# Distances between steps counted by the pieces' time, the first MLP's chain in three parts, and six seven-product groups more in the second MLP's down-projection

## The reference, cut to what matters

```python
def sq_relu_mlp(h, w1, w2):
    return jnp.square(jax.nn.relu(h @ w1)) @ w2                 # w1: 2048 x 8192
...
up = causal_dwconv(h @ w_up[l], conv_w[l], conv_b[l])           # w_up: 2048 x 11264, 3 taps
y = (jax.nn.gelu(up[..., :D_FF_2], approximate=True) * up[..., D_FF_2:]) @ w_down[l]   # w_down: 5632 x 2048
x = x + rms_norm_2(y, post_ffn_g[l])
```

## Time and profile before

| | us |
|---|---|
| median of 3 runs | 2083.37 (2083.08 to 2083.95) |
| the profiled execution, its own time | 2086.94 |
| its span, first to last instruction | 2085.2 |
| matmul engine busy | 2072.3 (99%), 9250 matmuls |
| VectorE busy | 1350.7 (65%) |
| ScalarE busy | 1117.5 (54%) |
| GpSimd busy | 118.6 (6%) |

### The profile page before, as it was taken

How to read it: one execution, slowest core, us unless ns; L and a number is a source line. 1 busy time by engine, 2 the same in 40 slices (tenths; PEclk the granted TensorE clock), 3 DMA queues, 4 the chain that set the end, 5 groups by cost and what they waited for, 6 DMA issues and landing times.

```text
span 2085.2 us, 23969 instructions
## 1 busy us (share of the span) xinstructions
PE 2072.3 (99%) x9250; PEld 1717.7 (82%) x9250; DVE 1350.7 (65%) x1504; ACT 1117.5 (54%) x1353; POOL 118.6 (6%) x66
## 2 busy tenths in 40 slices
PE   9999999999999999999999999999999999999998
PEld 7888888888888888888888888888888888888887
DVE  6546555666884579666876755566676765576665
ACT  7555654555554455455655554455555544555553
POOL 3000000000000000000002000000111100021110
PEclk9999999999999999999999999999999999999999
DMA  8687666788757776778677777667787756778763
GB/s 298 197 253 233 193 183 221 245 227 262 221 189 222 222 245 208 226 220 229 224 260 234 228 245 231 195 209 221 233 252 253 229 185 211 234 235 257 244 213 120
DMA packets 291906, 469.49 MB, mean 225 GB/s; under 512 B 18512, under 2 KB 82128, under 8 KB 291280
## 3 DMA queue, kind: packets, MB, share of 16 engines
q1 hardware_dynamic: 290928, 463.46, 72.2%
q10 hardware_dynamic: 864, 4.49, 0.6%
HBM read 432.75 MB, written 35.13 MB: 224 GB/s over the span
## 4 chain that ended last, share of the span: by engine, by line
PE 88%; DMA 5%; DVE 3%; ACT 2%; SPq 1%; issue 1%; ACTq 0%; DVEq 0%
PE ps L1734 88%; DMA T<-passed_strip 3%; DVE Wl L1340 1%; DMA passed_strip<-T 1%; DMA passed_rows<-xN 1%; SPq L1041 1%; ACT Wh L1116 1%; DVE T L1443 0%; DMA E<-passed_rows 0%; ACT hid L1219 0%; DVE xN L1469 0%; DVE T L1479 0%; PE ps L1737 0%; SPq L1030 0%; ACT T L1176 0%
## 5 line engine op out<-in xcount | busy, mean ns | idle before, releaser
L1340 DVE TENSOR_TENSOR Wl<-raw,Wh 128x1024 fp32r<-128x1024 f32 x743 | 919.7, 1258 | 565.1 <-ACT Wh L1116 559.7
L1734 PE MATMUL ps<-Wh,aHL 128*128 128x512 f32 x3712 | 1148.5, 390 | 2.1 <-DVE Wl L1335 0.9
L1116 ACT ACTIVATE Wh<-raw 128x1024 fp32r<-128x1024 f32 x743 | 771.5, 1057 | 551.8 <-PE ps L1734 527.8
L1734 PEld LDWEIGHTS ps<-Wh,aHL 128*128 128x128 f32 x3712 | 696.8, 188 | 147.5 <-DVE aHL L1483 1.2
L1734 PE MATMUL ps<-Wl,aHL 128*128 128x512 f32 x1856 | 722.1, 389 | 0.0
L1734 PE MATMUL ps<-Wh,hid 128*128 128x512 f32 x1548 | 480.7, 389 | 3.7 <-DVE Wl L1340 3.7
L1734 PEld LDWEIGHTS ps<-Wl,aHL 128*128 128x128 f32 x1856 | 348.5, 188 | 71.7
L1734 PEld LDWEIGHTS ps<-Wh,hid 128*128 128x128 f32 x1548 | 290.6, 188 | 64.8 <-issue 4.5
L1734 PE MATMUL ps<-Wl,hid 128*128 128x512 f32 x774 | 301.1, 389 | 0.0
L1734 PEld LDWEIGHTS ps<-Wl,hid 128*128 128x128 f32 x774 | 145.3, 188 | 30.1
L1734 PE MATMUL ps<-Wh,oHL 128*128 128x512 f32 x512 | 159.0, 390 | 0.0
(11 more groups left out here) (199 smaller groups left out, 923.0 us busy)
## 6 DMA issues: line engine op xcount, KB each, us to landing
raw<-in_mlp_w_dram SPq DMA_DIRECT2D x256, 512.0 KB, 5.5
raw<-in_w_up_dram SPq DMA_DIRECT2D x176, 512.0 KB, 4.5
raw<-in_sb_w_qkv_dram SPq DMA_DIRECT2D x93, 512.0 KB, 5.1
raw<-in_w_down_dram SPq DMA_DIRECT2D x88, 512.0 KB, 4.6
raw<-in_w_in_dram SPq DMA_DIRECT2D x64, 512.0 KB, 5.2
passed_strip<-T SPq DMA_DIRECT2D x104, 256.0 KB, 4.5
T<-passed_strip SPq DMA_DIRECT2D x208, 128.0 KB, 4.8
raw<-in_sb_w_o_dram SPq DMA_DIRECT2D x32, 512.0 KB, 5.6
```

The source lines that it names most:

```text
L1116: e.activation(Wh[:, i % NW, c], src, ACT.Copy).then_inc(st["hi"][0], 1)
L1340: e.tensor_tensor(Wl[:, i % NW, c], src, Wh[:, i % NW, c].bitcast(F32), ALU.subtract).then_inc(st["lo"][0], 1)
L1734: return e.matmul(o, l, r, start=start, stop=stop, skip_group_check=True)
```

## The change

Three edits. First, `later` counts time instead of pieces: an ordinary piece is four quarters, s0 to s2 are two each and s3 is one (`QUARTERS`), so that inside groups a distance of n spans more pieces. Second, the first MLP's chain: the turn comes one piece later (`behind` 5), and ScalarE's high half and VectorE's low half are steps of their own, each one piece further on. Third, in the second MLP three groups each in the first strip pair of both chunks: `sevens` is also set for s4 = 0, the token sums are also made in the second chunk, the number of ordinary pieces ahead of the first group is 2n - 5 (7 and 5) there and 4 in the second pair of the first chunk (before, 2), the first chunk's fold writes its results, the second's adds to them, and the last sums wait for the fold.

```diff
@@ -21,6 +21,7 @@
 BLOCKS = ((0, 0), (0, 1), (1, 1))
 SPANS = ((slice(0, 128), 0), (slice(128, 384), 4))
 ALL8 = tuple(range(8))
+QUARTERS = {"s0": 2, "s1": 2, "s2": 2, "s3": 1}
 
 
 class Plan:
@@ -47,7 +48,12 @@
         jobs.insert(0 if ahead else len(jobs), job)
 
     def later(self, n, job):
-        self.after(self.at + n, job)
+
+        i, left = self.at, 4 * n
+        while left > 0:
+            i += 1
+            left -= QUARTERS.get(self.pieces[i]["kind"], 4) if i < len(self.pieces) else 4
+        self.after(i, job)
 
 
 def plan_program(sem):
@@ -94,7 +100,7 @@
                                  start=(n == 0, n == 0), last=n == len(ks) - 1, evac=evac, early=None, strip=strips[0]))
         return first
 
-    def strip_pair(w, s4, ks, tail, mov, tiles, evacs, koff=0, sevens=(), fold=None):
+    def strip_pair(w, s4, ks, tail, mov, tiles, evacs, koff=0, sevens=(), fold=None, lead=None):
 
         plain = [kp for kp in ks if kp not in sevens]
         first, n = len(p.pieces), len(plain) - tail
@@ -105,8 +111,8 @@
             p.pieces[first:] = a[:n] + b[:n] + a[n:] + b[n:]
             return first
         b[0]["first"], b[0]["start"] = False, (False, True)
-        lead, gap = (4, 3) if tail else (2, 3 if len(plain) > 7 else 2)
-        rest = a[lead:n] + b[:n] if tail else a[lead:n - 1] + b[:2] + a[n - 1:] + b[2:]
+        lead, gap = (lead or 4, 3 if lead is None or len(plain) > 7 else 2) if tail else (lead or 2, 3 if len(plain) > 7 else 2)
+        rest = a[lead:n] + b[:n] if tail else a[lead:n - 1] + b[:lead] + a[n - 1:] + b[lead:]
         p.pieces[first:] = a[:lead]
         for m, kp in enumerate(sevens):
             seven(w, s4, kp, mov, tiles, (a[0]["strip"], b[0]["strip"]), koff, m, m == 0, fold if m == len(sevens) - 1 else None)
@@ -407,14 +413,23 @@
 
         def f(s, k):
             def landed(moved):
-                turned, hi, lo = done("hid_turned"), done("hid_hi"), done("hid_lo")
+                turned = done("hid_turned")
                 step("turn_strip", to="T1", need=[moved, *free["T1"]], done=turned)
-                step("hid_halves", t0=t0, need=turned, hi=hi, lo=lo)
-                free["T0"], free["T1"] = [turned], [lo]
+                free["T0"], free["T1"] = [turned], [turned]
+                later(1, lambda: high(turned))
+
+            def high(turned):
+                hi, lo = done("hid_hi"), done("hid_lo")
+                step("hid_high", t0=t0, need=turned, hi=hi)
+                free["T1"] = [lo]
+                later(1, lambda: low(turned, hi, lo))
+
+            def low(turned, hi, lo):
+                step("hid_low", t0=t0, hi=hi, lo=lo)
                 if mixed and t0 < 8:
                     free["T1"] = [lo, mix_tokens("hid1", "T1", t0 // 2, 2 if t0 == 0 else 1, [turned])]
                 hid_tiles[t0:t0 + 4] = [lo] * 4
-            trip(s, k, n, "relu", "b", [st["r2"]], landed)
+            trip(s, k, n, "relu", "b", [st["r2"]], landed, 5)
         return f
 
     def load_bias(s, k):
@@ -625,7 +640,7 @@
     MIXED_STRIPS = {0: (0, 2), 8: (2, 1)}
     conv_in = done("conv", 16)
 
-    def evac_conv(j, which, t0, last, at_first):
+    def evac_conv(j, which, t0, last):
         n = next_trip()
 
         def f(s, k):
@@ -666,7 +681,7 @@
                     hi, lo = done("hid_hi"), done("hid_lo")
                     step("gate_high", t0=t0, need=[g, *k], hi=hi)
                     free["E"] = [lo]
-                    if at_first and t0 in MIXED_STRIPS:
+                    if t0 in MIXED_STRIPS:
                         free["E"] = [lo, mix_tokens("hid2", "E", *MIXED_STRIPS[t0], [g])]
                     hid_tiles[t0:t0 + 4] = [lo] * 4
                     if last:
@@ -695,7 +710,8 @@
             for t in range(2):
                 y, q = done("y_summed"), done("y_squared")
                 g = done("y_gained") if s4 < 3 else done("y_gained_last")
-                kw = dict(t=t, s4=s4, set=s, mm=k[t], t0_free=list(free["T0"]), y=y, q=q, g=g, g_row=st["g_row"])
+                kw = dict(t=t, s4=s4, set=s, mm=k[t], t0_free=list(free["T0"]), y=y, q=q, g=g, g_row=st["g_row"],
+                          folded=st.get(("fold", s4)))
                 free["T0"] = [q]
                 st["yg", t, s4] = g
                 if s4 == 2:
@@ -725,14 +741,14 @@
     for c, n in enumerate((6, 5)):
         for j in range(n):
             for which in range(2):
-                i = strip("w_up_2", which * 5632 + (at + j) * STRIP, ALL8, "aHL", tile_hl, evac_conv(at + j, which, 4 * j, j == n - 1, c == 0))
+                i = strip("w_up_2", which * 5632 + (at + j) * STRIP, ALL8, "aHL", tile_hl, evac_conv(at + j, which, 4 * j, j == n - 1))
                 if at + j + which == 0:
                     after(i + 8, lambda: row_norm(into="r6"))
         for s4 in (0, 2):
             i = strip_pair("w_down_2", s4, tuple(range(2 * at, 2 * (at + n))), 0 if s4 else 2, "hid2", hid_tiles,
                            [evac_y(c, s4), evac_y(c, s4 + 1)], koff=2 * at,
-                           sevens=(2 * at, 2 * at + 1, 2 * at + 4) if c == 0 and s4 else (),
-                           fold=fold_into("xn", s4, fresh=True))
+                           sevens=(2 * at, 2 * at + 1, 2 * at + 4) if c == 0 or s4 == 0 else (),
+                           fold=fold_into("xn", s4, fresh=c == 0), lead=4 if s4 else 2 * n - 5)
             if c == 1 and s4 == 0:
                 after(i + 1, gain_rows)
                 after(i + 12, lambda: step("ready_sqrt", need=None))
@@ -1214,7 +1230,7 @@
                     g, oHL = st["g"], oHLs[st["blk"]]
                     e.wait_ge(*st["mm"])
                     e.activation(oHL[:, 4 * g:4 * g + 4, 0:TOK], ps[st["set"]][:, :, 0:TOK], ACT.Copy).then_inc(st["hi"][0], 1)
-                elif k == "hid_halves":
+                elif k == "hid_high":
                     e.wait_ge(*st["need"])
                     e.activation(hid1[:, st["t0"]:st["t0"] + 4, 0:TOK], T1[:, :, :], ACT.Copy).then_inc(st["hi"][0], 1)
                 elif k == "load_bias":
@@ -1502,7 +1518,7 @@
                 elif k == "keep_last":
                     cs = slice(3 * STRIP, 4 * STRIP)
                     e.tensor_tensor(xn[:, 1, cs], ps[st["set"]][:, 1, :], mixed_row[:, cs], ALU.mult).then_inc(st["kept"][0], 1)
-                elif k == "hid_halves":
+                elif k == "hid_low":
                     t0 = st["t0"]
                     e.wait_ge(*st["hi"])
                     e.tensor_tensor(hid1[:, t0:t0 + 4, TOK:2 * TOK], T1[:, :, :], hid1[:, t0:t0 + 4, 0:TOK].bitcast(F32),
@@ -1625,6 +1641,8 @@
                         e.wait_ge(*st["total"])
                         e.tensor_scalar(total, total, 1.0 / 2048, EPS, ALU.mult, ALU.add).then_inc(st["part"][0], 1)
                     e.wait_ge(*st["mm"])
+                    if st["folded"]:
+                        e.wait_ge(*st["folded"])
                     e.tensor_tensor(xn[:, t, cs], xn[:, t, cs], ps[st["set"]][:, t, :], ALU.add).then_inc(st["y"][0], 1)
                     if k == "y_last":
                         mean, r, y, h = moments(half)
```

## The result

The changed kernel takes 2090.39 us (median of 6 executions, 2089.42 to 2091.62), the kernel before 2083.21 beside it (6 executions, 2081.95 to 2083.95): 1.0036 of the time before, 95% interval 1.0025 to 1.0046. It is 7.2 us slower, where +3.3 was forecast with "within 0.2%" as the likeliest case. The profiled execution took 2089.46 us. For a profiled execution, from whose time before all 3.7 us of waits go, the forecast was 2088.4.

What follows compares the result with a forecast made beforehand. The matmul engine, busy 2072.3 of 2085.2 us, was taken as the bound. Terms: -4.1 matmuls, -1.9 first MLP, +5.8 second chunk, +2.5 first chunk, +1.0 clock = +3.3, so 2086.7 us; range 2080.0 to 2090.5.

Steps and rivals of the forecast that it cites:

- within 0.2%: Whole kernel: the forecast and what lies around it, within 4.2 us of before; chance 0.47.
- The matmuls: Second MLP, six more groups: 18 matmuls go at 0.227 us each, 4.1 us saved.
- The first MLP's waits on the median: First MLP: the new order removes waits for VectorE's Wl, 3.7 us in the profile; 1.9 gain taken on the median.
- The second chunk's wait: Second chunk's first pair: low half of hid2 comes late, matmuls wait 5.8 us; bounds 4.3 and 9.1.
- rival 1: Slower: second chunk's GpSimd gate kept out until VectorE stops at the low half, 3.3 us more, 2090.0; chance 0.40.
- The first chunk's wait: First chunk, around the third group: VectorE 0.4 us late plus 2.1 for GpSimd's gate, 2.5; bounds 0.4 and 3.8.
- The clock: Behind the second chunk's 5.4 us wait: half clock may cost 1.0 us; bounds 0 and 2.0.
- The rival "faster": VectorE keeps up, so only the savings stay: 2075.6 to 2079.3 us; needs the 4.3 lower bound wrong; chance 0.13.

Runs made afterwards that it cites:

- before_again: The kernel before, unchanged, measured once more: 2082.95 us; its profiled execution took 2082.79 us.
- low_together: first_mlp_only with the low half of hid1 again right behind its high half, one piece earlier: 2081.89 us, ratio 0.9994.
- first_mlp_only: The kernel before with the new distances and the first MLP's new chain, none of the six added groups: 2083.39 us, ratio 1.0001.
- chunk2_only: The changed kernel without the new groups of the first chunk's first pair, keeping the last chunk's: 2089.76 us, ratio 1.0032.
- lead_one: Changed kernel, last chunk's three groups in its second pair, behind one ordinary piece; two groups in the first chunk's first pair: 2080.76 us, ratio 0.9988.
- after_again: The changed kernel, unchanged, measured once more: 2091.27 us.
- chunk1_only: The changed kernel without the new groups of the second chunk, keeping those of the first chunk's first pair: 2084.11 us, ratio 1.0005.
- fold_behind: The changed kernel with the fold of the last chunk's first pair one piece later, behind the low half of hid2: 2091.80 us, ratio 1.0040.
- chunk2_two: The changed kernel with two groups instead of three in the last chunk's first pair: 2090.80 us, ratio 1.0034.
- table_late: chunk2_two with ScalarE's load of the sqrt table eight pieces later: 2089.37 us, ratio 1.0030.

## Why the prediction was wrong

Set beside before_again's execution, which has no waits for Wl or hid1 in the first MLP, after's span is 6.3 us longer (2087.3 against 2081.0): the matmul engine is busy 2.4 less (2069.9 against 2072.3) and idle 8.7 more. New waits are 8.0 of it: 5.05 for hid2, 2.26 for Wl, 0.7 for hid1. Another 0.6 stands at Wl L1351 in the first 7 us, but the small matmuls of the start are busy 0.6 less there (4.02 us against 4.63), so that it costs nothing. 18 matmuls less give -4.1, the half pace +1.5. That makes 5.4; five stops, each some 0.2 to 0.3 dearer than its row (an estimate from the rows under low_together), make 6.4 to 6.9, against the 6.3 measured. Outside the span after has 0.4 more. With the second dip of 1.7 in half of after's executions the difference is 6.7 to 8.4, and 7.2 is what was measured.

- **The matmuls**, -4.1: right.
- **The first MLP's waits on the median**, "I take the middle, 1.9": this step failed. The prediction saw itself that the profiled execution stood above the median by as much as these waits, and took half of them all the same. An execution near the median had none of them (before_again), and the new chain added two waits for hid1, 0.7 us by their rows and 1.3 in time: first_mlp_only is 0.6 above before, where 1.9 below was forecast. 2.5 us of the error, with the noise of its interval. What was to be had is seen in low_together, the same without the hid1 waits: 0.8 below before, and even that is within its interval.
- **The second chunk's wait**, 5.8: 5.2 (5.05 and the 0.16 in front of it). The tally of VectorE's queue held to half a us, and so did the gate beside the fold, which rival 1 would have kept out.
- **The first chunk's wait**, 2.5: 2.1.
- **The clock**, 1.0: the mechanism was right, the size was not. The dip behind the long wait costs 1.5 in after's profile and 2.7 in chunk2_only's, above the bound of 2.0. That bound was drawn from the program's start, and wrongly: the windows of before read 1.00 there from the first us on, so the start shows no stretch at half clock. And the 2.1 us wait lowers the clock too in about half of the executions, where I had priced none because a wait of 2.8 us before had left it full, though the earlier trace rows show it falling behind one of 2.26 us. Together 0.5 to 2.2 us of the error. The Trainium skill (TensorE: Matmul & The Clock Gate, Why this matters for your kernels) warns of long idle gaps between bursts of matmuls. These rows agree for the long wait; the 2.1 us gap is shorter than those that the page warns of, and was enough in some executions.

These terms make 2.5 - 0.6 - 0.4 + 0.5 to 2.2, that is 2.0 to 3.7 of the 3.9 us between forecast and result. The prediction also priced each wait at its length alone; by the estimate above the three stops in the two pairs cost 0.6 to 0.9 more.

"Within 0.2%" had 0.47 because the first MLP's gain was to pay for part of the waits; without it the same sum gives +5.2, and slower would have been the forecast. The rival "faster" fails on its own condition: the lower bound of the second chunk's wait, 4.3, held.

## What to carry to other kernels

Price a gain that exists only in the profiled execution at nothing when this execution is slower than the median by just that gain: the median execution hasn't got it. A saving in matmuls that is bought with vector work pays only where the vector engine has room: the same three groups cost 5.2 us beside a chain of filters and nothing in the next pair once they stood one piece earlier (lead_one). And a wait of the matmul engine costs more than its length: 0.27 us more for one of 0.38, and 1.5 to 2.7 us more where the pace behind it was halved.

## What the runs showed of the hardware

- The same wait of 2.1 us in the first chunk left the clock full in after's profile and was followed by half clock in after_again, chunk1_only, fold_behind, chunk2_two and table_late; before's 2.8 us wait left it full. Behind the long waits, 4.4 to 6.0 us, half clock followed in every profile, behind those of 5.05 us for 3.0 us of matmuls in one (after) and 5.4 in another (chunk2_only).
- A stop of 0.38 us in the stream of matmuls cost 0.65 us from start to start (first_mlp_only), since a row's idle time leaves out the overlap that is lost on both sides.
- GpSimd's gate got in at a sum of VectorE that depends on the sum just before it (the row at 1660.93 starts 0.04 us behind its predecessor's end): this sum took 2.77 us instead of 0.69 and GpSimd ran on. It was the same sum in after_again and chunk1_only (2.78 us); that the dependence is the reason was not tested. Five splits in sequence left no such place in 5.7 us.
